# Last feed-forward stage, blocks 4 to 20: products of 128 rows as two of 64 rows on two row tiles of TensorE

## The reference, cut to what matters

```python
h2 = rmsnorm(x, norm2_w)
a, v = jnp.split(h2 @ ffn_w_up, 2, axis=-1)          # 1024 -> 2 x 2816
a = gelu(causal_dwconv(a, ffn_conv_w, ffn_conv_b))   # 3 taps along the tokens
return x + (a * v) @ ffn_w_down                      # 2816 -> 1024
```

## Time and profile before

| what | value |
|---|---|
| median of 3 runs | 1409.92 us |
| the profiled execution, its own time | 1409.55 us |
| its span, first to last instruction | 1407.8 us |
| around the span | 1.75 us |
| TensorE busy (matmul) | 1402.0 us, x7632 |
| VectorE busy | 1089.5 us, x1650 |
| ScalarE busy | 862.1 us, x1397 |
| granted TensorE clock | 1.00 in every slice |

### The profile page before, as it was taken

How to read it: one execution, slowest core, us unless ns; L and a number is a source line. 1 busy time by engine, 2 the same in 40 slices (tenths; PEclk the granted TensorE clock), 3 DMA queues, 4 the chain that set the end, 5 groups by cost and what they waited for, 6 DMA issues and landing times.

```text
span 1407.8 us, 20193 instructions
## 1 busy us (share of the span) xinstructions
PE 1402.0 (100%) x7632; PEld 1194.9 (85%) x7632; DVE 1089.5 (77%) x1650; ACT 862.1 (61%) x1397; POOL 230.4 (16%) x307
## 2 busy tenths in 40 slices
PE   9999999999999999999999999999999999999999
PEld 7888888898888888888888888888888899888887
DVE  7878876676978878788775778788777877678776
ACT  6657656755667647576567646666567665455553
POOL 1112233000111001112050001114149200100000
PEclk9999999999999999999999999999999999999999
DMA  9999754454999859998563557999546335456551
GB/s 368 303 300 281 224 210 166 139 193 182 303 258 288 212 186 311 264 282 214 196 222 131 179 180 269 268 272 266 186 148 240 135 135 181 161 174 217 196 181 59
DMA packets 84049, 305.49 MB, mean 217 GB/s; under 512 B 9328, under 2 KB 9456, under 8 KB 83824
## 3 DMA queue, kind: packets, MB, share of 16 engines
q1 hardware_dynamic: 69840, 253.07, 50.6%
q0 software_dynamic: 13824, 50.34, 18.7%
q10 hardware_dynamic: 288, 0.79, 0.1%
HBM read 303.11 MB, written 1.05 MB: 216 GB/s over the span
## 4 chain that ended last, share of the span: by engine, by line
PE 98%; DVE 1%; DMA 0%; ACT 0%; issue 0%; POOL 0%; DVEq 0%; ACTq 0%; POOLq 0%
PE bank L720 18%; PE bank L727 9%; PE bank L674 9%; PE bank L675 9%; PE bank L676 9%; PE bank L880 5%; PE bank L879 5%; PE bank L883 5%; PE bank L741 4%; PE bank L746 4%; PE bank L742 4%; PE bank L704 3%; PE bank L711 3%; PE bank L705 3%; PE bank L694 1%; PE bank L973 1%
## 5 line engine op out<-in xcount | busy, mean ns | idle before, releaser
L1943 DVE TENSOR_TENSOR wlo<-raw,whi 128x1024 fp32r<-128x1024 f32 x409 | 492.2, 1231 | 12.3 <-ACT whi L1336 12.2
L1336 ACT ACTIVATE whi<-raw 128x1024 fp32r<-128x1024 f32 x409 | 417.5, 1048 | 16.7 <-PE bank L676 10.4
L720 PE MATMUL bank<-hx,whi 128*128 128x512 f32 x1088 | 269.7, 393 | 0.0
L720 PEld LDWEIGHTS bank<-hx,whi 128*128 128x128 f32 x1088 | 200.0, 188 | 41.7 <-issue 3.0
L674 PE MATMUL bank<-whi,hid 128*128 128x512 f32 x536 | 211.1, 394 | 0.0
L675 PE MATMUL bank<-wlo,hid 128*128 128x512 f32 x536 | 209.2, 390 | 0.0
L676 PE MATMUL bank<-whi,hid 128*128 128x512 f32 x536 | 208.8, 389 | 0.0
L727 PEld LDWEIGHTS bank<-hx,wlo 128*128 128x128 f32 x1088 | 143.0, 191 | 7.7
L727 PE MATMUL bank<-hx,wlo 128*128 128x256 f32 x1088 | 145.3, 282 | 0.0
L1943 DVE TENSOR_TENSOR wlo<-gates,whi 128x1024 fp32r<-128x1024 f32 x96 | 116.3, 1225 | 5.6 <-ACT whi L1336 5.2
L676 PEld LDWEIGHTS bank<-whi,hid 128*128 128x128 f32 x536 | 100.6, 188 | 21.4
(11 more groups left out here) (300 smaller groups left out, 2377.8 us busy)
## 6 DMA issues: line engine op xcount, KB each, us to landing
raw<-w_dram SPq DMA_DIRECT2D x414, 512.0 KB, 4.4
gates<-w_dram POOLq DMA_DIRECT2D x64, 512.0 KB, 8.0
gates<-w_dram SPq DMA_DIRECT2D x32, 512.0 KB, 5.4
arena<-w_dram POOLq DMA_DIRECT2D x32, 512.0 KB, 9.0
arena<-w_dram SPq DMA_DIRECT2D x16, 512.0 KB, 5.1
gain<-g_dram SPq DMA_DIRECT2D x7, 512.0 KB, 3.3
arena<-c_dram SPq DMA_DIRECT2D x2, 768.0 KB, 6.2
cst<-c_dram SPq DMA_DIRECT2D x1, 1056.0 KB, 8.4
```

The costliest lines, as they stand in the source:

```text
L720: e.matmul(b[:, :], hi_of(j)[:, k * P:k * P + P], hx[:, k * 2 * S:k * 2 * S + 2 * S], start=k == 0, stop=False, skip_group_check=True)
L1336: e.activation(hi_of(t), raw_of(t), ACT.Copy).then_inc(sem["w_hi"], 1)
L1943: e.tensor_tensor(lo_of(t), raw_of(t), hi_of(t).bitcast(F32), ALU.subtract).then_inc(sem["w_lo"], 1)
```

## The change

Blocks 4 to 20 call a new function `row_tiled`. Each product over 128 rows becomes a pair over rows 0 to 63 (row tile at 0) and 64 to 127 (row tile at 64). The two halves of a pair work on different output banks: in the first round the upper half serves tile a and the lower half tile b, and in the second round they change banks, so that each bank gets both halves. The down projection does the same with the two halves of the 1024 output columns. A new semaphore `rows`, counted by TensorE and waited for by TensorE, keeps a row tile from writing a bank before the other is through with it. The three tiles of a block are released together, by `tile` + 3 after the last product. The leads of these blocks' tiles are set to 5, 4 and 3 on both engines.

```diff
+for _i in range(4, 21):
+    HI_LEAD.update({f"Mfa{_i}": 5, f"Mfb{_i}": 4, f"Mfd{_i - 3}": 3})
+    LO_LEAD.update({f"Mfa{_i}": 5, f"Mfb{_i}": 4, f"Mfd{_i - 3}": 3})
...
+            def row_tiled(s, i, ja, jb, ba, bb):
+
+                h_ = K.HID0[s] + i - 3
+                jd, hb = T[K.HIDTILE[h_]], hid[h_ % 4]
+
+                def pair(b0, s0, m0, b1, s1, m1, first=False, last=False):
+                    e.matmul(b0, s0[0:64], m0[0:64], start=first, stop=last, tile_position=(0, 0), skip_group_check=True)
+                    return e.matmul(b1, s1[64:P], m1[64:P], start=first, stop=last, tile_position=(64, 0), skip_group_check=True)
+
+                def highs(j0, b0, j1, b1, first):
+                    for k in range(KD):
+                        m = hx[:, k * 2 * S:k * 2 * S + 2 * S]
+                        ins = pair(b0[:, :], hi_of(j0)[:, k * P:k * P + P], m, b1[:, :], hi_of(j1)[:, k * P:k * P + P], m, first and k == 0)
+                    return ins
+
+                def lows(j0, b0, j1, b1, last=False):
+                    for k in range(KD):
+                        ins = pair(b0[:, 0:S], lo_of(j0)[:, k * P:k * P + P], hiT(k), b1[:, 0:S], lo_of(j1)[:, k * P:k * P + P], hiT(k),
+                                   last=last and k == KD - 1)
+                    return ins
+
+                def sums(a, h):
+                    b0, b1 = side[2 * a + h][:, :], side[2 * a + 1 - h][:, :]
+                    s_hi, s_lo = hb[:, a * P:a * P + P], hb[:, S + a * P:S + a * P + P]
+                    part = lambda t, q: t[:, q * 512:q * 512 + 512]
+                    pair(b0, s_hi, part(hi_of(jd), h), b1, s_hi, part(hi_of(jd), 1 - h))
+                    pair(b0, s_lo, part(hi_of(jd), h), b1, s_lo, part(hi_of(jd), 1 - h))
+                    return pair(b0, s_hi, part(lo_of(jd), h), b1, s_hi, part(lo_of(jd), 1 - h))
+
+                t = 4 * (i - 4)
+                E.wait_ge("w_hi", SI[jb] + 1)
+                highs(ja, ba, jb, bb, True).then_inc(sem["rows"], 1)
+                wait_tile(jd)
+                E.wait_ge("hidlo", h_ + 1)
+                if i > 4:
+                    E.wait_ge("rows", t)
+                sums(0, 0)
+                sums(1, 0).then_inc(sem["rows"], 1)
+                E.wait_ge("rows", t + 1)
+                highs(jb, bb, ja, ba, False)
+                E.wait_ge("w_lo", SI[jb] + 1)
+                lows(jb, bb, ja, ba).then_inc(sem["rows"], 1)
+                E.wait_ge("rows", t + 2)
+                sums(0, 1)
+                sums(1, 1).then_inc(sem["rows"], 1)
+                E.wait_ge("rows", t + 3)
+                lows(ja, ba, jb, bb, True).then_inc(sem["tile"], 3)
...
                     if 3 < i < NF - 1:
-                        ba, bb = claim((tag, "a", i)), claim((tag, "b", i))
-                        high_part(ja, ba)
-                        high_part(jb, bb)
-                        low_part(ja, ba)
-                        low_part(jb, bb)
-                        accum(s, i - 3)
+                        row_tiled(s, i, ja, jb, claim((tag, "a", i)), claim((tag, "b", i)))
                         continue
```

More of the change, by code:

```diff
@@ L520, in build_program @@
         PES = ["tile", "tok", "xt", "ft", "acc", "qkt_t", "pl_d", "pl_w", "score", "pT", "pv",
-               "kT_t", "lg_row", "lg_col", "c_hT", "c_w2", "c_rep", "c_sc", "c_pT", "pv_c", "ml_m", "ml_s", "ml_h", "ml_t", "turn"]
+               "kT_t", "lg_row", "lg_col", "c_hT", "c_w2", "c_rep", "c_sc", "c_pT", "pv_c", "ml_m", "ml_s", "ml_h", "ml_t", "turn", "rows"]
         ACTS = ["w_hi", "sq", "xhi", "tok_a", "act", "hidhi", "pad", "qk_ev", "hst_sq", "kt_ev", "qt_ev", "u_ev", "v_ev", "dT", "yphi", "ex", "g_low",
```

## The result

The changed kernel takes **1422.29 us** (median of four runs, 1421.64 to 1422.69) against 1409.86 for the kernel before in the four runs beside it: ratio 1.0087, 95% interval 1.007 to 1.0105. That is slower by 12.4 us. The forecast was 1419.0, inside a range of 1413.5 to 1424; the time is 3.3 us above the forecast. The profiled execution took 1421.64, so 12.1 us more than that of before.

A forecast was written before the change was run, and what follows sets the result against it. ScalarE and VectorE's ring, 8.49 us a block, would bind the stage. Last 30 products start 9.2 us later (4.7 drift and entry, 4.5 last chain): 1409.55 + 9.2 = 1418.8, median 1419.0; range 1413.5 to 1424.

The forecast's parts named there:

- The pair: TensorE, blocks 4 to 20: half products run side by side, so a block stays 8.28 us, between bounds 7.75 and 8.81.
- third rival: Faster: row tiles hide the gap between products, 7.75 us a block, and ScalarE and VectorE keep up: 1404 to 1406; 7%.
- the double gap: TensorE pays the gap between products once for each half, 8.81 us a block: 1423 in all; chance 9%.
- the short ring: ScalarE and VectorE's cycle slightly shorter than TensorE's block, so only entry and end cost: some 1414; chance 8%.
- Entry and exit of the row tiles: TensorE, switching to row tiles and back: one entry and one exit, 0.4 us in all, lying in slack.
- The ring: ScalarE and VectorE: chain of a block, three splits, next chain take 8.49 us, 0.21 above TensorE's block, and bind the stage.
- first rival: The same as the short ring: only entry and end cost, some 1414; chance 8%.
- the release: Tile a's release moves from 4.6 us into the block to its end, 3.7 us later, using up ScalarE's 1.58 us slack.
- The last chain: Block 21's chain starts after block 20's end: first sum of block 20 at 1394.6, last 30 products at 1406.8; costs 4.5 us.
- The entry: Stage start: block 4's first VectorE sum moves from 1257.58 to 1258.72; TensorE first stalls in block 5, by 1.6 us.
- The clock: TensorE pauses twice for about 2 us before the last products; a clock fall there would come on top, unpriced.

The follow-up runs named there:

- experiment 4: Changed kernel with leads 5, 5, 5 in place of 5, 4, 3, row tiles and late release kept: 1417.73 us, ratio 1.0056.
- experiment 7: Changed kernel with leads 5, 5, 5, low products after high ones in each round, tiles a and b released before the last sums: 1413.19 us.
- experiment 8: As experiment 7, with tile `Mfd1` also split early, during block 2: 1412.12 us, ratio 1.0017.
- Experiment 1: Kernel before with only the leads 5, 4, 3 added; products, order and release untouched: 1418.99 us, ratio 1.0065.
- experiment 2: Changed kernel with whole 128-row products in place of the pairs and no `rows` waits; order, leads and release kept: 1420.36 us.
- experiment 3: Changed kernel run once more without any edit, for its spread and a second profile: 1421.42 us, ratio 1.0082.
- experiment 5: Changed kernel without its three lines on leads, so 5 on ScalarE and 4 on VectorE as before: 1453.34 us, two runs.
- experiment 6: Changed kernel with high and low part of `Mfd1` split early, during block 2: 1420.05 us, ratio 1.0072.

## Why the prediction was right

**The pair: right.** "Unchanged, 8.28" measured 8.31 where TensorE sets the pace (experiments 4, 7, 8), and 0.227 and 0.12 from pair to pair. The rule of the Trainium skill, page "TensorE: Matmul & The Clock Gate", Part 3, "What overlaps and what doesn't", that only loads for other row groups overlap running matmuls, would have given 7.75 as the prediction read it. No run shows a gain: the pairs load on alternating row tiles and go no faster than whole products do. The third rival falls with it, and so does the double gap (8.81). The times of two rivals were added up a little short: the terms of the short ring give 1414.7 and not "some 1414", those of the double gap 1423.7 and not 1423. It changes nothing in the range.

**Entry and exit of the row tiles: right, and in slack.** Between the last full product (1247.94) and the first pair (1248.26) lie 0.32 us, to the second pair 0.34: about 0.2 above two steps of 0.23. At the exit, in experiment 8, the first full product starts 0.35 us after the last pair (1389.43 and 1389.78) instead of 0.23, and the eight full high products with it last 2.12 instead of 2.00: 0.2 again. It shows in the time only where TensorE binds.

**The ring: right to 0.01 us.** 8.49 in sixteen steps, with the same pieces that the forecast added up. Experiment 1 shows that the leads make it, without any row tile or late release. The shorter ring of the first rival, with some 1414, is excluded.

**Who causes it: the forecast put too much on the release.** It named the late release and the leads together, and explained 4.5 us at the end by tile a being released at the end of block 20. Experiment 1 has the old release and loses the same 9.24 us. Under leads of 5, 4, 3 the release costs nothing on top, since the ring decides. Under leads of 5, 5, 5 the row tiles and the late order cost 7.9 us (experiment 4), of which another order with an earlier release returns 4.5 (experiment 7). Part of both figures is the clock: it fell twice in the profiled execution of experiment 4 and in no run of experiment 7. No run has the late release with whole products and these leads, so its own price stays open. The prices don't add up: each edit alone has one, together they have little more than the larger.

**The last chain: right.** From the first sum of block 20 to the last 30 products it takes 1409.61 - 1397.27 = 12.34, where the forecast had 1406.8 - 1394.6 = 12.2.

**The step that failed: the entry.** The forecast moved block 4's first sum to 1258.72, from VectorE's own queue, and placed the first stall of TensorE in block 5, at 1257. It didn't check the same question a block earlier: block 4's sums are due after 8 pairs too, and the low part of `Mfd1` wasn't there. TensorE stood idle for 2.19 us. By experiment 2 that alone would have cost nothing: there the gap is 2.43, the clock holds, and the last products start at the same 1406.86 as with the leads alone. In the profiled execution the clock fell behind it, about 8 pairs took 0.2 us more each, and VectorE's first sum comes at 1261.41, 1.6 later than 1258.72 and the 1.1 lost upstream would give. The account: 9.2 predicted + 1.6 + 1.1 = 11.9 of the 12.0 measured at the last products. The second profiled execution (experiment 3) adds up the same way: 9.2 + 1.6 at block 4 + 0.3 upstream = 11.1 of 11.2, and 1.6 more within the last 30 products.

**The clock: named, not priced.** The forecast said that a fall of the clock would come on top of 1419.0. Of the eight runs of the changed kernel the one with a mean clock of 1.000 took 1419.42, and the others 1.0 to 3.5 us more. So the forecast of 1419.0 met the program with its clock held. The 3.3 us between forecast and median are what the clock and the loss upstream took in the two executions that were profiled; for the other six that is argued from their mean clocks. The forecast had looked for pauses at the end alone, and its own width, 1416.5 to 1421, does not reach the median. The stated range does because it was made wide for two rivals that did not come true: that part is luck.

**The loss upstream: not the change.** Against first sums of block 2 at 1237.48 it was 1.1 us in the first profiled execution of the changed kernel, 0.3 in its second one, 1.2 in experiment 5, 0.6 in 6, 0.4 in 8, and nothing (0.06 at most) in experiments 1, 2, 4 and 7. All of it has arisen by 190 us, a thousand us ahead of the changed stage, in code that is the same in all of them. The 0.3 is there from the start: VectorE's first operation waits for the first load until 4.97 us instead of 4.69. The three largest come mostly from one place near 141.7 us, where a VectorE add of 512 columns starts almost together with one on GpSimd. The kernel before, then the changed one:

```profile
141.55 0.69 DVE L2070 TENSOR_TENSOR arena<-arena 128x512 f32<-128x512 f32 x1 [0.80 <-ACT arena L1427]
141.57 2.02 POOL L2622 TENSOR_TENSOR arena<-cst,par 128x32 f32<-128x32 f32 x1
```

```profile
141.72 2.73 DVE L2116 TENSOR_TENSOR arena<-arena 128x512 f32<-128x512 f32 x1 [0.80 <-ACT arena L1473]
141.74 0.58 POOL L2668 TENSOR_TENSOR arena<-cst,par 128x32 f32<-128x32 f32 x1
```

VectorE's add takes 2.74 and 2.73 us in experiments 5 and 6 too, and 0.69 in the profiled executions of all the others. Where it is the long one, the program comes out of this place some 0.9 us later.

**Left open:** why the clock falls behind one gap and not behind another, and what decides which of the two adds is the long one.

## What to carry to other kernels

An in-order engine that prepares data ahead has a ring: chain of a step, preparation, chain of the next. Add it up before changing how far ahead it works, for a change that leaves it 0.2 us longer than the busy engine's step costs that at every step, while the busy engine still shows 99%. A pause of TensorE that is itself free can bring on a fall of its clock, and the fall costs time where others wait for TensorE next. When a consumer is moved forward within a step, ask for each of its inputs in the first step of the loop too, not only in a steady one. Two half-height products on two row tiles are one whole product in time, so cutting a full-height product in two gained nothing here; in the earlier trace rows the height is 64 to begin with, and a pair does two products at a time.

## What the runs showed of the hardware

A pair of 64-row products in the rounded format, on row tiles 0 and 64 and into two banks, takes the 0.227 us (512 columns) or 0.12 us (256 columns) of one 128-row product. How far its halves lie apart makes no difference: they start together in block 4, and 0.05 apart at 1290.

The clock fell to one half behind idle stretches of TensorE of the same size as others behind which it held. In block 4 of the changed kernel and of experiment 4 it fell behind 2.19 us without a matmul, in experiment 2 it held behind 2.43. At the end it held behind 1.80 in the changed kernel's first profiled execution and fell behind 1.82 in its second. Within one execution (experiment 5) it fell behind 2 of 16 pauses of 1.76 or 1.77. The same program, the changed kernel, spreads over 3.5 us, where the kernel before, without such pauses, stays within 0.7 (1409.37 to 1410.03 in the runs beside these experiments), and experiments 7 and 8, whose longest wait of TensorE in this stage is 0.75, within 0.9 and 0.6, all at 1.000.

Where a VectorE add of 512 columns and GpSimd adds ran at the same time (at 141.7 us), one side took its time and the other was long: 0.69 us on VectorE beside 2.02 on GpSimd, or 2.73 beside 0.58. Which side it was differs between executions of code that is the same there, with starts 0.02 to 0.03 apart in either case. That the two engines hold each other up fits this; no run separates them.
